# A transformer layer on one core: head 0's first eight picks from the best eight keys of each half, and tile 1's columns turned behind the out-projection

## The reference, cut to what matters

```python
qc = (rms_norm(x1) @ w_query).reshape(C, 8, 2, 128)          # 8 heads, 2 halves
s = einsum('chpd,hpnd->chpn', qc, sub_keys)                   # 128 keys in each half
top_s, top_i = top_k(s, 16)                                   # per half
cand_s = top_s[:, :, 0, :, None] + top_s[:, :, 1, None, :]    # 16 x 16 sums
cand_i = top_i[:, :, 0, :, None] * 128 + top_i[:, :, 1, None, :]
best_s, best_pos = top_k(cand_s, 16)
expert_idx = take_along_axis(cand_i, best_pos)                # 16 experts of 16384
act = gelu(einsum('chkd,cd->chk', expert_u[expert_idx], xc))
out = einsum('chk,chkd->cd', softmax(best_s) * act, expert_v[expert_idx])
```

## Time and profile before

| | before |
|---|---|
| median of 3 runs | 1776.05 us (1775.26 to 1777.1) |
| the profiled execution's own time | 1772.37 us |
| its span in the trace | 1770.7 us |
| granted TensorE clock, mean | 0.835 of full |
| PE busy | 1265.6 us (71%) |
| DVE busy | 1288.6 us (73%) |
| ACT busy | 347.3 us (20%) |
| POOL busy | 824.9 us (47%) |
| DMA moved | 634.42 MB, mean 358 GB/s |

### The profile page before, as it was taken

How to read it: one execution, slowest core, us unless ns; L and a number is a source line. 1 busy time by engine, 2 the same in 40 slices (tenths; PEclk the granted TensorE clock), 3 DMA queues, 4 the chain that set the end, 5 groups by cost and what they waited for, 6 DMA issues and landing times.

```text
span 1770.7 us, 12898 instructions
## 1 busy us (share of the span) xinstructions
PE 1265.6 (71%) x3980; PEld 702.9 (40%) x3980; DVE 1288.6 (73%) x1752; ACT 347.3 (20%) x645; POOL 824.9 (47%) x546
## 2 busy tenths in 40 slices
PE   9999999999927565666766556666755666556567
PEld 7888887778913221122322112323311212121112
DVE  5555656456797778787878778787878787887674
ACT  5333444554011010110101111101101111101001
POOL 1000000000476556555466576655576566575553
PEclk9999999999967877778788778778877767777779
DMA  8886556178799999999999999999999999999997
GB/s 240 214 211 193 170 167 202 37 243 271 302 421 420 420 420 421 421 421 420 420 422 421 422 418 423 421 422 421 421 418 422 422 417 422 421 405 423 423 421 313
DMA packets 131361, 634.42 MB, mean 358 GB/s; under 512 B 13491, under 2 KB 26373, under 8 KB 65509
## 3 DMA queue, kind: packets, MB, share of 16 engines
q0 software_dynamic: 74384, 538.74, 73.5%
q1 hardware_dynamic: 56884, 94.94, 17.5%
q10 hardware_dynamic: 32, 0.01, 0.0%
HBM read 631.29 MB, written 2.36 MB: 358 GB/s over the span
## 4 chain that ended last, share of the span: by engine, by line
DMA 47%; PE 35%; issue 6%; POOL 5%; DVE 5%; ACT 1%; POOLq 0%; DVEq 0%; ACTq 0%
DMA more_rows<-in_peer_expert_v,pick_row 26%; PE ps L1857 10%; DMA big<-in_peer_expert_v,pick_row 9%; DMA big<-in_peer_expert_u,pick_row 7%; PE ps L1455 6%; PE ps L1457 6%; PE ps L1456 6%; DMA more_rows<-in_peer_expert_u,pick_row 5%; PE ps L1833 2%; POOL big L601 2%; POOL more_rows L601 2%; DVE big L1367 2%; DVE more_rows L1367 1%; POOL more_rows L596 1%; PE ps L1528 1%
## 5 line engine op out<-in xcount | busy, mean ns | idle before, releaser
L1857 PE MATMUL ps<-big,diag 128*128 128x512 f32 x512 | 358.5, 840 | 248.8 <-DMA big<-in_peer_expert_v,pick_row 185.4
L1857 PE MATMUL ps<-more_rows,diag 128*128 128x512 f32 x512 | 349.7, 820 | 240.9 <-DMA more_rows<-in_peer_expert_v,pick_row 240.9
L1367 DVE CUSTOM_DVE_ANT_0 more_rows<-more_rows,big 128x2048 f32<-128x2048 f32 x130 | 297.9, 2293 | 123.6 <-DMA more_rows<-in_peer_expert_u,pick_row 122.6
L1367 DVE CUSTOM_DVE_ANT_0 big<-big 128x2048 f32<-128x2048 f32 x126 | 288.6, 2293 | 104.3 <-DMA big<-in_peer_expert_u,pick_row 104.3
L601 POOL DMA_INDIRECT big<-in_peer_expert_v,pick_row x128 | 213.9, 1671 | 210.7 <-PE ps L1857 166.4
L1857 PEld LDWEIGHTS ps<-big,diag 128*128 128x128 f32 x512 | 116.2, 249 | 474.7 <-DMA big<-in_peer_expert_v,pick_row 304.8
L601 POOL DMA_INDIRECT more_rows<-in_peer_expert_v,pick_row x128 | 220.4, 1722 | 179.6 <-PE ps L1857 120.8
L1857 PEld LDWEIGHTS ps<-more_rows,diag 128*128 128x128 f32 x512 | 111.0, 238 | 461.0 <-DMA more_rows<-in_peer_expert_v,pick_row 372.0
L824 ACT ACTIVATE diag<-ident,pick_w 128x128 f32<-128x128 f32 x256 | 96.6, 396 | 826.8 <-PE ps L1857 595.8
L866 DVE TENSOR_TENSOR split_lo<-raw,split_hi 128x1024 fp32r<-128x1024 f32 x119 | 145.8, 1225 | 145.0 <-ACT split_hi L625 119.4
L596 POOL DMA_INDIRECT more_rows<-in_peer_expert_u,pick_row x130 | 189.4, 1457 | 56.4 <-issue 37.2
(11 more groups left out here) (247 smaller groups left out, 989.4 us busy)
## 6 DMA issues: line engine op xcount, KB each, us to landing
raw<-in_w_in SPq DMA_DIRECT2D x88, 512.0 KB, 3.7
raw<-in_w_out SPq DMA_DIRECT2D x32, 512.0 KB, 4.9
big<-in_peer_w_query SPq DMA_DIRECT2D x16, 512.0 KB, 6.6
raw<-in_peer_w_query SPq DMA_DIRECT2D x8, 512.0 KB, 7.7
spare<-in_peer_w_query SPq DMA_DIRECT2D x8, 512.0 KB, 9.0
more_rows<-in_peer_expert_u,pick_row POOLq DMA_INDIRECT x130, 16.5
big<-in_x SPq DMA_DIRECT2D x4, 512.0 KB, 7.9
raw<-in_cmp_k_w SPq DMA_DIRECT2D x4, 512.0 KB, 6.1
```

The costliest lines, as they stand in the source:

```text
L1367: dve.tensor_tensor_reduce(row, row, XN[:, place_of(m // TOPK)[0], :], 1.0, 0.0, ALU.mult, ALU.add, pick_dot[:, m:m + 1]).then_inc(dotted, 1)
L1857: ins = pe.matmul(psf[:, t * V_PE + c:t * V_PE + c + 512], diag[:, m % DIAGS, :], row[:, c:c + 512], start=m == first, stop=m == picks_to( ...
```

## The change

Four parts. (1) Head 0: the best eight keys of each half give 64 sums, and from these come the first eight picks and their rows. The replacement in the scores and the next eight keys come behind them, after last x1 of tile 1; there all 256 sums are formed, with the 64 (in which the eight best are replaced) copied into their corner. (2) PE turns tile 1's chunks 0 to 2 behind the out-projection, between pieces of the query projections; ACT copies their columns there. (3) Only the last out-projection step runs by tile. (4) The spare places are filled in the order 0, 2, 1, 3, and the first two wait for one step less.

```diff
-LAST_STEPS = SPLIT
+LAST_STEPS = 1
...
-            return ("raw", "spare", "ahead")[i // RAW] + str(i % RAW)
+            return ("raw", "spare", "ahead")[i // RAW] + str((0, 2, 1, 3)[i % RAW] if i // RAW == 1 else i % RAW)
...
-                elif m == RAW:
-                    sp.wait_ge(split_free, SP_END + SPLIT)
+                elif m in (RAW, RAW + 2):
+                    sp.wait_ge(split_free, SP_END + SPLIT - (m == RAW))
...
-                if p in X1_TURNED:
-                    x1_columns(X1_TURNED[p])
...
-            x1_columns(W_CHUNKS - 1)
+                for c in range(2 * h, 2 * h + 2):
+                    x1_columns(c)
...
+            def first_keys(v, scores):
+                for s in range(2):
+                    step(dve.max(head_top[:, s, v], scores(s)))
+                after()
+                for s in range(2):
+                    step(dve.max_index(head_topi[:, s, v], head_top[:, s, v], scores(s)))
+                after()
+                step(dve.tensor_scalar(head_topf[:, 0, v], head_topi[:, 0, v], float(NKEYS), None, ALU.mult))
+                step(dve.tensor_copy(head_topf[:, 1, v], head_topi[:, 1, v]))
...
-            for part in range(6):
-                head_part(0, part)
-            first_rows(0)
+            first_keys(lo8, lambda s: score_at(0, s))
+            sums_of(first_sums, 8)
+            best_of(lo8, first_sums)
+            first_rows(0, 8)
+            for s in range(2):
+                step(dve.match_replace(head_s[:, s, :], head_top[:, s, lo8], score_at(0, s), -3.0e38))
             last_x1(1)
             x1_gained(W_CHUNKS - 1, 1)
...
+            step(dve.match_replace(first_sums, head_best[:, lo8], first_sums, -3.0e38))
+            after()
+            first_keys(hi8, lambda s: head_s[:, s, :])
+            sums_of(head_sums, TOPK)
+            after()
+            step(dve.tensor_copy(head_sums.rearrange("p (a b) -> p a b", a=TOPK)[:, lo8, lo8], first_sums.rearrange("p (a b) -> p a b", a=8)))
+            best_of(hi8, head_sums)
...
+            first_rows(1, TOPK)
...
-                    for t in range(TT):
-                        turn_x1(0, t)
+                    turn_x1(0, 0)
...
                 if head == 1:
-                    pe.wait_ge(head_step, 6)
+                    pe.wait_ge(sem("first_step"), FIRST_READ)
...
-            out_tile(len(OUT_ORDER) - 2, 0)
-            first_queries(0, 0, 0, 0, 2)
             out_tile(len(OUT_ORDER) - 1, 0).then_inc(sem("last_out"), 1)
-            first_queries(0, 0, 0, 2, KC // 2)
+            first_queries(0, 0, 0, 0, 4)
             turn_x1(W_CHUNKS - 1, 0)
-            first_queries(0, 0, 0, KC // 2, KC).then_inc(sem("first_queries"), 1)
-            out_tile(len(OUT_ORDER) - LAST_STEPS, 1, (0,))
+            first_queries(0, 0, 0, 4, KC).then_inc(sem("first_queries"), 1)
+            out_tile(len(OUT_ORDER) - 1, 1, (0,))
             head_scores(0)
-            out_tile(len(OUT_ORDER) - LAST_STEPS, 1, (1,)).then_inc(split_free, 1)
-            for p in range(len(OUT_ORDER) - LAST_STEPS + 1, len(OUT_ORDER)):
-                out_tile(p, 1).then_inc(split_free, 1)
-            first_queries(1, 0, 2).then_inc(sem("first_queries"), 1)
+            out_tile(len(OUT_ORDER) - 1, 1, (1,)).then_inc(split_free, 1)
+            turn_x1(0, 1)
+            first_queries(1, 0, 2, 0, KC // 2)
+            turn_x1(1, 1)
+            first_queries(1, 0, 2, KC // 2, KC).then_inc(sem("first_queries"), 1)
+            turn_x1(2, 1)
             head_scores(1)
+            first_queries(0, 1, 1, 0, KC // 2)
             turn_x1(W_CHUNKS - 1, 1)
-            first_queries(0, 1, 1)
+            first_queries(0, 1, 1, KC // 2, KC)
```

More of the change, by code:

```diff
@@ L96 @@
 HEAD_OPS = 26
+FIRST_READ = 17
 QUERY_FIRST = STEPS_PER_CHUNK
@@ L1333, in _, with step, after, first_rows @@
             first_step = [0]
[L1335 to L1343, removed]
-                v = slice(8 * half, 8 * half + 8)
[L1346 to L1351, removed]
+            def step(ins):
+                first_step[0] += 1
+                ins.then_inc(sem("first_step"), 1)
+            def after():
+                dve.wait_ge(sem("first_step"), first_step[0])
+            def first_rows(half, keys):
+                v = slice(8 * half, 8 * half + 8)
+                after()
+                step(dve.tensor_scalar(head_ab[:, 0, v], head_pos[:, v], 4 if keys == TOPK else 3, None, ALU.logical_shift_right))
+                step(dve.tensor_scalar(head_ab[:, 1, v], head_pos[:, v], keys - 1, None, ALU.bitwise_and))
                 after()
@@ L1363, in first_rows, with sums_of, best_of @@
                 dve.tensor_tensor(pick_row[:, v], head_row[:, 0, v], head_row[:, 1, v], ALU.add).then_inc(sem("first_rows"), 1)
+            def first_keys(v, scores):
[7 more added lines that the diff above has]
+                step(dve.tensor_copy(head_topf[:, 1, v], head_topi[:, 1, v]))
+            def sums_of(out, n):
+                step(dve.tensor_tensor(out.rearrange("p (a b) -> p a b", a=n), head_top[:, 0, 0:n].unsqueeze(2).broadcast_to([P, n, n]),
+                                       head_top[:, 1, 0:n].unsqueeze(1).broadcast_to([P, n, n]), ALU.add))
+            def best_of(v, sums):
+                after()
+                step(dve.max(head_best[:, v], sums))
+                after()
+                step(dve.max_index(head_pos[:, v], head_best[:, v], sums))
             def pick_dot_of(m):
@@ L1794, in _ @@
                     pe.wait_ge(sem("keys_ready"), 2)
-                    for t in range(TT):
-                        turn_x1(0, t)
+                    turn_x1(0, 0)
                 if p == 21:
-                    for t in range(TT):
-                        turn_x1(1, t)
+                    turn_x1(1, 0)
                 if p == 28:
-                    for t in range(TT):
-                        turn_x1(2, t)
+                    turn_x1(2, 0)
                 out_step(p)
@@ L1838, in head_scores @@
                 if head == 1:
-                    pe.wait_ge(head_step, 6)
-                if head >= 4:
+                    pe.wait_ge(sem("first_step"), FIRST_READ)
+                if head == 4:
+                    pe.wait_ge(head_step, HEAD_OPS)
+                if head > 4:
                     pe.wait_ge(head_step, (head - 4) * HEAD_OPS + 6)
```

23 lines of the change are left out of this document (12 added, 11 removed).

## The result

The changed kernel takes 1776.21 us (median of 22 runs, 1773.72 to 1781.64), the kernel before beside it 1774.55: ratio 1.0017, 95% interval 1.0011 to 1.0023, so 3.0 us slower, which is clear of noise and still inside the 0.2% that I called no change. My range, 1769.8 to 1775.2, doesn't hold it, and the forecast gain of 4.1 us didn't come. The profiled execution has a span of 1774.2 us and lies at 1775.97.

What follows compares the result with a forecast made beforehand. The second stage was taken as bound by DMA volume over rate, so only time ahead of the first gather counts: -0.40 - 2.96 - 0.75 = -4.1 us, giving 1772.0 us; own range 1770.5 to 1773.2, wider range 1769.8 to 1775.2.

Steps and rivals of the forecast that it cites:

- PE up to the first scores: Out-projection to head 0's scores: fewer transposes, more matmuls in step 30 and no wait for the last split, -0.40 us.
- DVE from scores to rows: Head 0's scores to its first eight pick rows: passes removed or shortened, 6.80 to 3.84 us, -2.96 us.
- DMA: where the stream starts: First gather's bytes: spare query loads finish sooner and hold them back less, -0.75 us beyond the earlier issue.
- the first rival: Spare loads held the first gather back altogether, its own delay being 1.1 us: -5.0 us, 1771.0 us; chance 0.13.
- It holds, by 0.6 us: At gather 12, 3.0 us of DMA backlog against at most 2.4 us to first byte keeps the stream fed.
- The balance of bytes: Loads asked for minus bytes moved until gather 12's issue: 2.5 MB open, 6.1 us of backlog before the change.
- PE's term, -1.0 us: PE's work up to gather 12's issue, with matmuls removed and turns added: about 1.0 us earlier.
- mostly hidden by a turn (-0.45): Ahead of head 1's scores, a turn covers most of PE's 0.57 us wait for ACT, -0.45 us.
- None should stop PE: Turns of tile 1 between query projections: 3.6 us of queries cover each of ACT's 1.14 us column copies.
- the lead is lost at gather 12: Two turns wait openly for ACT, PE comes 3.4 us later, 2.8 us lost: 1774.7 us; chance 0.15.
- Slower issues: Gathers 0 to 11 each take 3.0 us to issue, DMA starves 8.9 us: 1780.9 us; chance 0.05.
- The sum as a whole: Whole kernel: the PE, DVE and DMA terms together give -4.1 us, 1772.0 us at the median.

Runs made afterwards that it cites:

- behind_late: scores_behind with the first gather held back about 3 us by a wait for five more VectorE steps; ratio 1.0004 to the kernel before.
- scores_behind: The changed kernel with head 1's scores put behind the first half of tile 1's query projection; ratio 0.9980 to the kernel before.
- pad_64: The changed kernel with 64 empty TensorE instructions at its start; ratio 1.0021 to the kernel before, with the start padded.
- pad_160: The changed kernel with 160 empty TensorE instructions at its start; ratio 1.0115 to the kernel before, with the start padded.
- plain_first: The changed kernel with its first eight gathers replaced by plain loads of 128 consecutive rows, so its output differs; ratio 0.9982 to the kernel before.
- pad_256: The changed kernel with 256 empty TensorE instructions at its start; ratio 1.0222 to the kernel before, with the start padded.
- fill_53: The changed kernel with 53 empty TensorE instructions laid into waits that PE has anyway; 1777.54 us, ratio 1.0014 to the kernel before.

## Why the prediction was wrong

- **PE up to the first scores, -0.40 us**: from the first turn (402.73 before, 403.04 after) to the scores on DVE pass 47.79 and 47.51 us, so -0.28. Right in kind; the execution's own offset of 0.3 us hid it.
- **DVE from scores to rows, -2.96 us**: -2.97 measured between the scores and gather 0 (+7.08, +4.11). Right. The passes over 64 elements took 0.22 and 0.23 us.
- **DMA: where the stream starts, -0.75 us**: mis-sized, the term is -0.1. The first packet follows the issue by 1.82 us in the changed kernel, 1.91 before, and 1.80 in behind_late, where nothing is in front; so the spare loads held back next to nothing of a gather as late as before's, and the first rival (own delay 1.1 us) falls as well. I had read the loads as over by 460 us and the gather as starting behind them; in the trace of before their last packet comes at 461.28 and the gather's first at 459.51, side by side. The lead was 3.0 us, not 4.1, and 2.95 of it last to the last gather in scores_behind. Gather 0's last landing, with gather 1 issued 1.4 us behind it, is recorded 5.97 and 5.71 us behind its issue in pad_64 and pad_160 (6.65 before). The Trainium skill's fit ("DMA: Bandwidth & Descriptors", "Anatomy of one DMA") made it 4.4, and the measurement decides.
- **Gather 12, "It holds, by 0.6 us"**: the step that failed. The balance of bytes was right: by it the stream runs dry at 491.8 us with 4.1 us of lead, so at 492.9 with 3.0, and it did at 492.8. Wrong was PE's term, -1.0 us: it became +6.5, of 3.62 us for head 1's scores that start late and 2.88 for the clock. The part of it that failed is the wait of the second scores for ACT, "mostly hidden by a turn (-0.45)", which leaves 0.12 us: it measured 4.22. The cover there was one turn of 0.6 us, and the hand-over was taken from the kernel before. "None should stop PE" spoke of the turns, with 3.6 us of queries between them, and those didn't stop it. That the account of PE was otherwise sound is shown by pad_64 and plain_first (+38.77, +38.75 against my +38.7). 3.6 us of cover would have been nearly enough: in scores_behind PE stands 1.04 us.
- **Rival "the lead is lost at gather 12"**: its place was right, its mechanism (two turns waiting openly for ACT, 3.4 us) was not; the loss went beyond it. I had no term for the clock. By an estimate from the rows above, the stop alone would have put gather 12 at 493.4 and its bytes 1.8 to 2.8 us behind (first packets of gather 0, and of gather 12 here), 2.4 to 3.4 us later than the stream wants them: about the whole lead of 3.0. pad_256, with the same stop and half the clock loss, comes between: gather 12 at +44.48, the last gather at +1298.07.
- **Slower issues**: the first six went out 1.3 us apart, where I had about 1.4, and none but gather 6 (2.74 us) took over 2 us up to gather 11.
- **The sum as a whole**: its two terms up to gather 0 were nearly right, -3.25 of -3.36 us. The miss of the time lies behind gather 0, in a wait of PE that the account left at 0.12 us.

What stays open: by what means TensorE's signals come 4 us late, what the gathers and a shift of TensorE's program have to do with each other in it, and why the signals come free at a fixed distance from gather 0. ACT's waiting copy starts 8.69 to 8.80 us behind it in all ten kernels with the early gather and a late signal, and 8.07 to 8.15 us in the three with the late one. A version with 64 instructions spread where they cost nothing wasn't tried.

## What to carry to other kernels

A lead is kept only where the next dependent issue has slack; count that slack against the slowest hand-over, and give a wait on another engine ready work in front of it, also where the profile shows that wait at half a microsecond: here 32 query records (3.6 us of work) moved ahead of one wait turned +3.0 us into -3.5. A stop of TensorE is to be priced with the clock behind it: 3.6 us more of standing cost 2.9 us on top here, 1.6 in pad_256. And when a change that should gain doesn't, shift the program without changing the work (empty instructions) before the change is blamed: the same change put gather 12 at +45.7 or +38.8 us by that alone.

## What I had not expected of the hardware

TensorE's hand-over to ScalarE, under 0.02 us beyond the recorded end in the kernel before, took 3.6 to 4.2 us at one place in ten kernels with the early gather, and was as short as before with 64 or 160 instructions more at the start of TensorE's program or with plain loads in the gathers' place. In the same kernels most landing records of the first gather are missing. An empty TensorE instruction that counts up a semaphore takes 0.154 us: PE's idle time at the start is 7.43, 22.10 and 37.02 us with 64, 160 and 256 of them. (The 0.138 us of fill_53's expectation divided 22.10 by 160, but the first of them run beside 2.4 us of matmuls.)
